# Column sums of the latent norms and of a layer norm: from fp32 columns and a root on four numbers per row to split fp32r products with ones and a root on whole tiles

## The chip, the cores and the metric

One of the eight cores of a Trainium2 chip runs the whole program in one launch. The metric is the device time of that launch in microseconds (us); lower is better. The kernel before took 3165.73 us (median of 3 runs, 3165.16 to 3166.70). Engines are named as in the profile: PE is TensorE (matmuls) and PEld its weight loads, ACT is ScalarE, DVE is VectorE, POOL is GpSimd, SP is the queue that issues most of the DMAs.

## The reference

Four blocks run one after the other on 512 positions of 1024 channels. In the first two (below: layers 0 and 1) a convolution branch is layer-normed over its 512 channels; in the last two (layers 2 and 3) an attention branch normalises two latent vectors, of 384 and of 256 channels, by their root mean square before they are projected to queries, keys and values.

```
c = causal_dwconv(glu, cf_conv_w[l], cf_conv_b[l])
c = jax.nn.silu(layernorm(c, cf_ln_g[l], cf_ln_b[l]))       # 512 channels, layers 0 and 1
...
q = (rmsnorm_2(c_q, q_norm_g) @ w_uq)                       # 384 channels, layers 2 and 3
kv = (rmsnorm_2(c_kv, kv_norm_g) @ w_ukv)                   # 256 channels
```

## The kernel before

Activations lie with channels on the 128 partitions and the 512 positions along a row, so each of these norms is a sum over partitions. `F(n)` is an fp32 tile of 128x512, `R(n)` the same room read as fp32r, the fast matmul type; `R(hi)` and `R(lo)` hold a value rounded to fp32r (`hi_part`, a CAST on ACT, L1052) and the rest (`lo_part`, a subtraction on DVE, L1455). Each weight chunk of up to 128x1024 comes by DMA into `raw`, ACT casts it into `wh` (`cut`, L977), DVE writes the rest into `wl` (`cut`, L1445), and PE then multiplies three products for each 128x128 block: high with high, high with low, low with high.

The order on each engine is the order in which its program is written. It runs over the weight chunks, and `slot(name)` marks a chunk: on ACT and on DVE it first cuts the chunk two further on (`LA`), then runs what the table `BESIDE` has for this chunk, and only then comes the chunk's own work. In layers 2 and 3 the chunks around the change are, in this order: `ckv1`, `kr`, `zb0`, `zb1`, `qr0`, `qr1`, `vb0`, `vb1`, `qk0`, `zb2`. `qr0` and `qr1` multiply the normed 384 channels, `vb0` and `vb1` the normed 256. `gate_head` takes a `zb` group through Tanh (ACT, L1233) and a product (DVE, L1832). The results of `qr0` and `qr1` are rotated: SP issues a `swap` of each (four small DMAs, L2215), but in its queue that stands behind the wait for the low part of an earlier chunk: the swaps of rows 0 and 1 wait for `vb1` to be cut. DVE multiplies what was swapped (L1687), POOL combines (L2106, L2109), and ACT and DVE split the result for `scores(0)`, the first score products of the attention.

A norm's sum before: POOL adds the squares of the tiles into one, `columns` multiplies it by a column of ones in fp32 (four matmuls with one output column each), DVE scales and adds EPS (`col`, L1460), POOL takes the power -0.5 of 4 numbers per partition (`root`, L2049), and `rows` spreads them over all partitions by four fp32 matmuls with the identity. DVE then multiplies by what lies in PSUM (L1519 for the latents, L1505 for the layer norm). The layer norm's mean is one fp32 matmul with ones.

Of the kernel before, what the change touches and what calls it, by code (L numbers as in the profile page):

```python
# [12 lines left out]
P = 128  # L13
# [334 lines left out]
BESIDE_LN = ("ln_sum", "ln_centre", "ln_root")  # L348
# [24 lines left out]
def build(nc, x_in, wst, vec, cst, tab, gmb, gains_in, out):  # L373
    ctx = ExitStack()
    with ctx:
# [14 lines left out]
        ct = sb("ct", [P, 2, P], F32)  # L390
        sm = sb("sm", [P, 160], F32)
# [3 lines left out]
        half = sm[:, 144:160]  # L395
# [104 lines left out]
        def tensor(e, w):  # L500
# [41 lines left out]
            def columns(key, tiles, wait):  # L542

                o = take(key)
                w.wait_ge(*at("landed", "cst"))
                w.wait_ge(*wait)
                last = None
                for n, a in enumerate(a[:, t * P:(t + 1) * P] for a in tiles for t in range(a.shape[1] // P)):
                    last = mm(o[:, n:n + 1], a, ones[:, 0:1], True, True)
                last.then_inc(*group_done.up(("done", key)))  # L550

            def rows(key, r, c0, n, at_col, wait):

                o = take(key)
                w.wait_ge(*at("landed", "cst"))
                w.wait_ge(*wait)
                for t in range(n):
                    last = mm(o[:, at_col + t * P:at_col + (t + 1) * P], r[:, c0 + t:c0 + t + 1].to_broadcast([P, P]),
                              ident, True, True)
                last.then_inc(*group_done.up(("done", key)))  # L560

            def small_step(what, L=None, i=None, j=None):
# [7 lines left out]
                elif what == "ln_centre":  # L570
                    o = take(("lnm", L))
                    w.wait_ge(*at("ln_sum", L))
                    mm(o, ones, F(62), True, True).then_inc(*group_done.up(("done", ("lnm", L))))
                elif what == "ln_root":
                    columns(("lcol", L), [F(62)], at("ln_added", L, 3))
                elif what == "ln_spread":
                    rows(("lrow", L), small(1), 0, NT, 0, at("root", "ln", L))
                elif what == "n_root":
                    columns(("ncol", L, i), [F(61 if i == "q" else 67)], at("n_added", L, i))
                elif what == "n_apply":  # L580
                    rows(("nrow", L, i), small(1 if i == "q" else 3), 0, NT, 0, at("root", "n" + i, L))
# [381 lines left out]
        def scalar(e, w):  # L963
# [20 lines left out]
            def small_step(what, L=None, i=None, j=None):  # L984
# [14 lines left out]
                elif what == "ln_centre":  # L999
                    for j in range(4):  # L1000
# [3 lines left out]
                        e.activation(F(62 + j), F(20 + j), ACT.Square).then_inc(*act_square.up(("ln_square", L, j)))  # L1004
# [8 lines left out]
                elif what == "n_squares":  # L1013
                    tiles, acc, tmp = ((47, 48, 49), 61, (62, 63)) if i == "q" else ((50, 51), 67, (68,))
                    for n, f in enumerate(tiles):
                        w.wait_ge(*at("copied", L, f))
                        if n == 0:
                            e.activation(F(acc), F(f), ACT.Square).then_inc(*act_square.up(("n_square", L, i, 0)))
                        else:
                            e.activation(F(tmp[n - 1]), F(f), ACT.Square).then_inc(  # L1020
# [193 lines left out]
            def mixer2(L):  # L1214
# [13 lines left out]
                def gate_head(h):  # L1228
                    key = f"{L}/zb{h}"
                    w.wait_ge(*at("done", key))  # L1230
                    if h == 7:
                        w.wait_ge(*at("done", ("ncol", L, "k")))
# [186 lines left out]
            cut(3)  # L1419
            for L in (0, 1):  # L1420
# [7 lines left out]
        def vector(e, w):  # L1428
# [28 lines left out]
            def col(key, n, D, q, event):  # L1457

                w.wait_ge(*at("done", key))
                e.tensor_scalar(q[:, 0:n], bank(key)[:, 0:n], 1.0 / D, EPS, ALU.mult, ALU.add).then_inc(  # L1460
                    *dve_col.up(event, ("free", key)))

            def small_step(what, L=None, i=None, j=None):
# [28 lines left out]
                elif what == "ln_centre":  # L1492
                    key = ("lnm", L)
                    w.wait_ge(*at("done", key))
                    for j in range(4):
                        e.scalar_tensor_tensor(out=F(20 + j), in0=bank(key), scalar=-1.0 / 512, in1=F(20 + j),
                                               op0=ALU.mult, op1=ALU.add).then_inc(
                            *dve_tile.up(("ln_centred", L, j), ("free", key)))
                elif what == "ln_root":
                    col(("lcol", L), NT, 512, small(0), ("col", "ln", L))  # L1500
                elif what == "ln_out":
                    key = ("lrow", L)
                    C, q = F(20 + i), F(63 + i % 2)
                    w.wait_ge(*at("done", key))
                    e.scalar_tensor_tensor(out=C, in0=C, scalar=vec1(L, "lng", i)[:, 0:1], in1=bank(key), op0=ALU.mult,  # L1505
                                           op1=ALU.mult).then_inc(*dve_tile.up(("ln_scaled", L, i), ("free", key)))
# [4 lines left out]
                elif what == "n_root":  # L1511
                    col(("ncol", L, i), NT, 384 if i == "q" else 256, small(0 if i == "q" else 2), ("col", "n" + i, L))
                elif what == "n_apply":
                    key = ("nrow", L, i)
                    n, src, hi, lo, tmp, gain = (3, 47, 32, 35, (64, 65, 66), "qg") if i == "q" else \
                        (2, 50, 38, 40, (55, 56), "kvg")
                    w.wait_ge(*at("done", key))
                    for k in range(n):
                        e.scalar_tensor_tensor(out=F(tmp[k]), in0=F(src + k), scalar=vec2(L, gain, k)[:, 0:1],  # L1519
                                               in1=bank(key), op0=ALU.mult, op1=ALU.mult).then_inc(  # L1520
                            *dve_tile.up(("n_scaled", L, i, k), ("free", key)))
# [865 lines left out]
```

## Time and profile before

| what | value |
|---|---|
| median of 3 runs | 3165.73 us |
| the profiled execution's own time | 3166.51 us |
| its span in the profile | 3165.1 us |
| PE busy | 3145.4 us, 99% of the span |
| DVE, ACT, POOL busy | 1833.1, 1241.2, 395.9 us |
| granted PE clock | 1.00 |

The span is from the first to the last recorded instruction; the time has 1.4 us more around it. Matmuls overlap their successors, so the cost of one to PE is the distance between the starts of two, not its recorded duration.

### The profile page before, as it was taken

How to read it: one execution, taken by the hardware profiler on the slowest of the kernel's cores; microseconds unless marked ns; L12 is line 12 of the kernel's file. 1: busy time of each engine (PE TensorE's matmuls, PEld its weight loads, DVE VectorE, ACT ScalarE, POOL GpSimd, SP SyncE). 2: the span in 40 equal slices, each digit the busy share in tenths (PEclk: the TensorE clock that was granted, in tenths of full speed). 3: DMA queues.
4: the chain of work that ended last, by engine and by line, in shares of the span. 5: the costliest groups of instructions: out<-in, count | busy, mean ns of one | idle time of the engine just before them, and what ended most of it. 6: DMA issues, size and time to landing. Idle time of an engine off the chain costs nothing.

```text
span 3165.1 us, 36907 instructions
## 1 busy us (share of the span) xinstructions
PE 3145.4 (99%) x14844; PEld 2632.5 (83%) x14844; DVE 1833.1 (58%) x2493; ACT 1241.2 (39%) x1866; POOL 395.9 (13%) x293
## 2 busy tenths in 40 slices
PE   8999999999999999999999999999999999999999
PEld 7888888888888888888888888888888888888887
DVE  5875456655687545666557643447645754344754
ACT  3332334344433234434445432226634543223742
POOL 0201212110020111111012000110011100011001
PEclk9999999999999999999999999999999999999999
DMA  4322223235432223222542222223432222222422
GB/s 163 122 93 100 93 100 107 93 111 201 149 120 100 88 99 113 94 94 100 206 139 82 86 96 91 96 93 113 129 132 72 82 93 93 87 100 94 140 98 102
DMA packets 105352, 345.47 MB, mean 109 GB/s; under 512 B 13824, under 2 KB 14080, under 8 KB 104416
## 3 DMA queue, kind: packets, MB, share of 16 engines
q1 hardware_dynamic: 101856, 328.53, 30.8%
q0 software_dynamic: 3184, 14.06, 1.2%
q8 instruction: 119, 1.95, 0.3%
q10 hardware_dynamic: 144, 0.52, 0.1%
q14 instruction: 49, 0.40, 0.0%
HBM read 324.71 MB, written 2.10 MB: 103 GB/s over the span
## 4 chain that ended last, share of the span: by engine, by line
PE 97%; DVE 1%; issue 1%; ACT 0%; DMA 0%; POOL 0%; POOLq 0%
PE ps L513 96%; PE ps L618 1%; PE ps L859 0%; DVE r L1455 0%; DVE wl L1445 0%; DMA X<-x_in 0%; POOL sm L2049 0%; ACT f L1286 0%; DVE h L1588 0%; DVE sm L1882 0%; PE ps L568 0%; DVE f L1581 0%; DVE f L1832 0%; DVE f L1892 0%; DVE r L1864 0%
## 5 line engine op out<-in xcount | busy, mean ns | idle before, releaser
L513 PE MATMUL ps<-h,wh 128*128 128x512 f32 (+1 forms) x5824 | 1703.9, 377 | 2.3 <-DVE h L1588 1.7
L513 PEld LDWEIGHTS ps<-h,wh 128*128 128x128 f32 x5824 | 1066.9, 189 | 201.5 <-issue 6.7
L513 PE MATMUL ps<-h,wl 128*128 128x512 f32 (+1 forms) x2912 | 1093.7, 376 | 0.0
L1445 DVE TENSOR_TENSOR wl<-raw,wh 128x1024 fp32r<-128x1024 f32 (+3 forms) x584 | 739.4, 1279 | 310.6 <-ACT wh L977 309.6
L977 ACT CAST wh<-raw 128x1024 fp32r<-128x1024 f32 (+2 forms) x596 | 591.3, 1004 | 705.4 <-PE ps L513 699.1
L513 PEld LDWEIGHTS ps<-h,wl 128*128 128x128 f32 x2912 | 549.3, 189 | 99.2
L513 PE MATMUL ps<-r,wh 128*128 128x512 f32 x1536 | 474.5, 390 | 0.0
L513 PEld LDWEIGHTS ps<-r,wh 128*128 128x128 f32 x1536 | 287.3, 188 | 59.0
L1052 ACT CAST r<-f 128x512 fp32r<-128x512 f32 x186 | 114.5, 620 | 495.9 <-DVE f L1785 148.5
L513 PE MATMUL ps<-r,wl 128*128 128x512 f32 x792 | 304.5, 389 | 0.0
L513 PE MATMUL ps<-wh,r 128*128 128x512 f32 x960 | 302.3, 390 | 0.3
L1675 DVE TENSOR_TENSOR f<-f,ps 128x512 f32<-128x512 f32 x96 | 66.0, 687 | 377.2 <-PE ps L513 377.1
L513 PEld LDWEIGHTS ps<-wh,r 128*128 128x128 f32 x960 | 180.2, 188 | 39.0 <-ACT r L977 1.9
L1455 DVE TENSOR_TENSOR r<-f,r 128x512 fp32r<-128x512 f32 (+1 forms) x212 | 150.3, 714 | 102.3 <-ACT r L1052 100.7
L2136 POOL TENSOR_TENSOR f<-f,f 128x512 f32<-128x512 f32 x64 | 114.5, 1790 | 746.1 <-DVE f L1675 746.1
L513 PE MATMUL ps<-wl,r 128*128 128x512 f32 x480 | 186.8, 389 | 0.0
L513 PE MATMUL ps<-r,r 128*128 128x512 f32 (+3 forms) x864 | 180.6, 361 | 0.0
L1777 DVE SCALAR_TENSOR_TENSOR f<-ps,vt,f 128x511 f32<-128x511 f32 (+1 forms) x176 | 131.4, 747 | 80.6 <-ACT f L1204 77.5
L1468 DVE SCALAR_TENSOR_TENSOR f<-f,vt,f 128x511 f32<-128x511 f32 (+26 forms) x240 | 175.3, 781 | 0.6
L513 PEld LDWEIGHTS ps<-r,wl 128*128 128x128 f32 x792 | 148.7, 188 | 31.3 <-DMA r<-r 0.3
L513 PEld LDWEIGHTS ps<-r,r 128*128 128x128 f32 x864 | 146.7, 188 | 21.6
L2161 POOL TENSOR_TENSOR f<-f,f 128x512 f32<-128x512 f32 x44 | 92.4, 2100 | 388.0 <-DVE f L1777 388.0
(155 smaller groups left out, 2099.6 us busy)
## 6 DMA issues: line engine op xcount, KB each, us to landing
raw<-wst SPq DMA_DIRECT2D x544, 512.0 KB, 3.3
raw<-wst SPq DMA_DIRECT2D x48, 320.0 KB, 2.8
r<-r SPq DMA_DIRECT2D x64, 128.0 KB, 2.3
f<-gains POOLq DMA_DIRECT2D x6, 1024.0 KB, 5.2
raw<-wst SPq DMA_DIRECT2D x20, 256.0 KB, 2.8
f<-f SPq DMA_DIRECT2D x72, 64.0 KB, 2.0
f<-tab POOLq DMA_DIRECT2D x16, 256.0 KB, 4.6
X<-x_in SPq DMA_DIRECT2D x4, 512.0 KB, 8.3
```

The costliest lines, as they stand in the source:

```text
L513: return e.matmul(o, a, b, start=start, stop=stop, skip_group_check=True)
L618: last = e.transpose(o[:, i * P:(i + 1) * P], F(H[a])[:, i * P:(i + 1) * P], ident)
L977: e.copy(h[:, 0:WIDTH[c]], raw[:, c % NRAW, 0:WIDTH[c]]).then_inc(*hi_cut.up(("hi", c)))
L1052: e.copy(r, f).then_inc(*act_hi.up(event))
L1445: e.tensor_tensor(l[:, 0:WIDTH[c]], raw[:, c % NRAW, 0:WIDTH[c]], h[:, 0:WIDTH[c]].bitcast(F32), ALU.subtract).then_inc(*lo_cut.up(("lo", c)))
L1455: e.tensor_tensor(lo, f, hi.bitcast(F32), ALU.subtract).then_inc(*dve_lo.up(event))
L1468: e.scalar_tensor_tensor(out=C, in0=F(16 + j)[:, 0:S - s], scalar=vec1(L, "cfw", 31 * j + i)[:, 0:1], in1=C, op0=ALU.mult, op1=ALU.add).th ...
L1675: e.tensor_tensor(F(M + j) if begins else q, q, bank(key), ALU.mult).then_inc(*dve_tile.up(("free", key), *events))
L1777: e.scalar_tensor_tensor(out=q[:, s:S], in0=bank(key)[:, 0:S - s], scalar=vec1(L, "fcw", 3 * (22 * m + j) + 2 - s)[:, 0:1], in1=q[:, s:S], ...
L2136: e.tensor_tensor(F(M + j), F(M + j), gate_at(L, b, j), ALU.add).then_inc(*pool_sum.up(*events))
L2161: e.tensor_tensor(F(t + 1), F(t), F(t + 1), ALU.mult).then_inc(*pool_tile.up(("f_prod", L, j)))
```

## The change

The sums over channels become products of the sum tile's high and low parts with a 128x128 tile of ones in fp32r (`spread_sum`, two matmuls of 512 columns each), which leave the sum on all partitions at once. The squares carry the 1/D already. ACT takes the square root of the whole 128x512 tile from PSUM with EPS as its bias, DVE takes the reciprocal of that tile, and the scaling on DVE reads it from SBUF. The single column matmuls, the matmuls with the identity, DVE's `col` and POOL's `root` of these norms go away; the split of each sum (one CAST on ACT, one subtraction on DVE) comes in. The layer norm's mean is summed in the same way. The table `BESIDE` has the steps at other chunks.

```
-        put(t, f"{L}/gate0_7", [[("ln_sum", L)], [], [("ln_centre", L)], [], [], [("ln_root", L)], [("ln_spread", L)]]
+        put(t, f"{L}/gate0_7", [[("ln_sum", L)], [("ln_split", L)], [("ln_centre", L)], [], [("ln_split2", L)], [("ln_root", L)], []]
...
-        put(t, f"{L}/ckv1", [[("n_squares", L, "q")], [("n_squares", L, "k")], [("n_root", L, "q")],
-                             [("n_apply", L, "q"), ("n_root", L, "k")], [("n_apply", L, "k")]])
+        put(t, f"{L}/ckv1", [[("n_squares", L, "q")], [("n_squares", L, "k"), ("n_split", L, "q")],
+                             [("n_split", L, "k"), ("n_root", L, "q"), ("n_apply", L, "q")],
+                             [("n_root", L, "k"), ("n_apply", L, "k")]])
...
+            def spread_sum(key, i, wait):
+
+                _, hi, lo = SUM_AT[i]
                 o = take(key)
...
+                mm(o, ones_r[:, :], R(hi), True, False)
+                mm(o, ones_r[:, :], R(lo), False, True).then_inc(*group_done.up(("done", key)))
...
+                elif what in ("ln_root", "n_root"):
+                    key, i = (("lrow", L), "ln") if what == "ln_root" else (("nrow", L, i), i)
+                    w.wait_ge(*at("done", key))
+                    w.wait_ge(*at("eps"))
+                    e.activation(F(SUM_AT[i][0]), bank(key), ACT.Sqrt, bias=eps).then_inc(
+                        *act_tile.up(("deviation", key), ("free", key)))
...
-            def col(key, n, D, q, event):
-
-                w.wait_ge(*at("done", key))
-                e.tensor_scalar(q[:, 0:n], bank(key)[:, 0:n], 1.0 / D, EPS, ALU.mult, ALU.add).then_inc(
-                    *dve_col.up(event, ("free", key)))
+            def root_all(key, q):
+
+                w.wait_ge(*at("deviation", key))
+                e.reciprocal(q, q).then_inc(*dve_col.up(("root",) + key))
...
-                elif what == "n_root":
-                    src, dst = (0, 1) if i == "q" else (2, 3)
-                    root(small(src), small(dst), NT, at("col", "n" + i, L), ("root", "n" + i, L))
```

ACT's program in layer 2, from the copy of `kr`'s result on. Before: the copy (`f_512_162`), the cut of `qr0`, the Tanh of `zb0`, the cut of `qr1`, the three high parts of the normed 384 channels, the Tanh of `zb1`, the cut of `vb0`.

```order
L1059 COPY f_512_162<-ps 128x512 [waits s_group_done]
L977 CAST wh<-raw 128x768 [waits s_raw0]
L1233 ACTIVATE f_512_151<-ps 128x512 [waits s_group_done]
L977 CAST wh<-raw 128x768 [waits s_raw1]
L1052 CAST r_512_56<-f_512_156 128x512 [waits s_dve_tile]
L1052 CAST r_512_64<-f_512_157 128x512 [waits s_dve_tile]
L1052 CAST r_512_69<-f_512_158 128x512 [waits s_dve_tile]
L1233 ACTIVATE f_512_163<-ps 128x512 [waits s_group_done]
L977 CAST wh<-raw 128x1024 [waits s_raw2]
```

In the changed kernel, from the same cut of `qr0` (L964 is now the cut, L1054 the high part, L1001 the root, L1235 the Tanh), up to the cut of `vb0`:

```order
L964 CAST wh<-raw 128x768 [waits s_raw0]
L1054 CAST r_512_70<-f_512_120 128x512 [waits s_pool_sum]
L1001 ACT_TABLE_LOAD
L1001 ACTIVATE f_512_62<-ps,sm 128x512 [waits s_group_done]
...
L1235 ACT_TABLE_LOAD
L1235 ACTIVATE f_512_151<-ps 128x512 [waits s_group_done]
L964 CAST wh<-raw 128x768 [waits s_raw1]
L1001 ACT_TABLE_LOAD
L1001 ACTIVATE f_512_120<-ps,sm 128x512 [waits s_group_done]
L1054 CAST r_512_70<-f_512_161 128x512 [waits s_dve_tile]
L1054 CAST r_512_74<-f_512_163 128x512 [waits s_dve_tile]
L1235 ACT_TABLE_LOAD
L1235 ACTIVATE f_512_164<-ps 128x512 [waits s_group_done]
L964 CAST wh<-raw 128x1024 [waits s_raw2]
```

The "..." are the three high parts of the 384 channels. Two roots, four loads of ACT's function tables, and the two high parts of the 256 channels now stand ahead of the cut of `vb0`; before, those two high parts came behind it. Layer 3 reads the same.

DVE's program at the same place, in the changed kernel, from the cut of `qr0` to the cuts of `vb0` and `vb1` (x2). L1459 is the low part, L1464 the reciprocal, L1527 the scaling, L1840 the product of `gate_head`.

```order
L1449 TENSOR_TENSOR wl<-raw,wh 128x768 [waits s_hi_cut]
L1459 TENSOR_TENSOR r_512_77<-f_512_120,r_512_70 128x512 [waits s_act_hi]
L1464 RECIPROCAL f_512_62<-f_512_62 128x512 [waits s_act_tile]
...
L1459 TENSOR_TENSOR r_512_65<-f_512_158,r_512_69 128x512 [waits s_act_hi]
L1840 SCALAR_TENSOR_TENSOR f_512_151<-f_512_151,ps 128x512 [waits s_act_tile]
L1449 TENSOR_TENSOR wl<-raw,wh 128x768 [waits s_hi_cut]
L1464 RECIPROCAL f_512_120<-f_512_120 128x512 [waits s_act_tile]
...
L1840 SCALAR_TENSOR_TENSOR f_512_164<-f_512_164,ps 128x512 [waits s_act_tile]
L1449 TENSOR_TENSOR wl<-raw,wh 128x1024 [waits s_hi_cut] x2
```

Before, a 128x4 TENSOR_SCALAR (L1460) stood in place of each reciprocal. Everything behind a reciprocal on DVE waits for it, the cut of `vb0` too.

## Rows read from the trace of the kernel before

**Rows 1.** The page: busy us, share of the span, instructions.

```profile
PE 3145.4 (99%) x14844; PEld 2632.5 (83%) x14844; DVE 1833.1 (58%) x2493; ACT 1241.2 (39%) x1866; POOL 395.9 (13%) x293
```

**Rows 2.** PE in time, layer 0, the layer norm's mean: start us, us.

```profile
278.12 1.02 PE L513 MATMUL ps<-f,ct 128*128 128x512 f32 x2
...
279.44 0.40 PE L513 MATMUL ps<-h,wl 128*128 128x512 f32 x1
```

**Rows 3.** PE in time, layer 2, a latent norm's columns and rows.

```profile
1657.86 0.95 PE L513 MATMUL ps<-ct,f 128*128 128x1 f32 x8
...
1659.22 0.40 PE L513 MATMUL ps<-h,wl 128*128 128x512 f32 x1
...
1670.58 0.39 PE L513 MATMUL ps<-h,wl 128*128 128x512 f32 x1
...
1671.26 0.39 PE L513 MATMUL ps<-h,wl 128*128 128x512 f32 x1
1671.85 1.13 PE L513 MATMUL ps<-ct,sm 128*128 128x128 f32 x8 [0.20 <-POOL sm L2049]
...
1673.29 0.40 PE L513 MATMUL ps<-r,wl 128*128 128x512 f32 x1
```

**Rows 4.** ACT and DVE in time, layer 0, behind the layer norm's columns.

```profile
301.99 2.00 ACT L977 CAST wh<-raw 128x1024 fp32r<-128x1024 f32 x2 [10.29 <-PE ps L513]
...
302.01 0.69 DVE L1675 TENSOR_TENSOR f<-f,ps 128x512 f32<-128x512 f32 x1 [7.22 <-PE ps L513]
```

**Rows 5.** DVE's reciprocals, by their two lines: ns min/median/max.

```profile
L1888 DVE RECIPROCAL sm<-sm x16: 177/178/179, 1710.1 to 2582.5; 128x4 f32<-128x4 f32 x16
...
L1805 DVE RECIPROCAL sm<-sm x2: 216/216/216, 1647.3 to 2416.9; 128x10 f32<-128x10 f32 x2
```

**Rows 6.** ACT in time, layer 2: a switch of function tables.

```profile
1645.28 0.21 ACT L1217 ACTIVATE sm<-vt 128x10 f32<-128x10 f32 x1
1645.50 1.28 ACT L1219 ACT_TABLE_LOAD   x1
1646.80 0.21 ACT L1219 ACTIVATE sm<-sm 128x10 f32<-128x10 f32 x1
```

**Rows 7.** Groups by line and shape: busy us, mean ns.

```profile
L1052 ACT CAST r<-f 128x512 fp32r<-128x512 f32 x186 | 114.5, 620 | 495.9 <-DVE f L1785 148.5 <-POOL f L2189 140.1 <-POOL f L2136 58.3
L1455 DVE TENSOR_TENSOR r<-f,r 128x512 fp32r<-128x512 f32 x188 | 129.9, 697 | 101.5 <-ACT r L1052 100.7 <-ACT r L1240 0.5
L1368 ACT ACTIVATE f<-ps,sm 128x512 f32<-128x512 f32 x20 | 13.8, 688 | 13.8 <-PE ps L513 7.6 <-DVE r L1455 6.1
L1508 DVE SCALAR_TENSOR_TENSOR f<-f,vt,f 128x512 f32<-128x512 f32 x8 | 6.0, 751 | 6.3 <-ACT f L1010 6.3
```

**Rows 8.** ACT and DVE in time, layer 2: the cut of `qr0`, and `vb0`'s two halves.

```profile
1658.54 0.84 ACT L977 CAST wh<-raw 128x768 fp32r<-128x768 f32 x1
...
1672.17 1.04 ACT L977 CAST wh<-raw 128x1024 fp32r<-128x1024 f32 x1
...
1673.25 1.23 DVE L1445 TENSOR_TENSOR wl<-raw,wh 128x1024 fp32r<-128x1024 f32 x1 [0.25 <-ACT wh L977]
```

**Rows 9.** SP and DVE in time, layer 2: the first swaps and what follows them.

```profile
1679.97 4.95 SPq L2215 DMA_DIRECT2D f<-f  x8
...
1683.84 0.69 DVE L1687 TENSOR_TENSOR f<-f,f 128x512 f32<-128x512 f32 x1 [0.54 <-DMA f<-f]
...
1699.02 1.28 DVE L1864 TENSOR_TENSOR r<-ps,r 128x512 fp32r<-128x512 f32 x2
```

**Rows 10.** PE in time, layer 2: the first scores, and the first values product.

```profile
1700.75 3.33 PE L513 MATMUL ps<-r,r 128*128 128x128 f32 x20
...
1717.41 1.96 PE L513 MATMUL ps<-f,f 128*128 128x512 f32 x5 [0.17 <-DVE f L1900]
```

**Rows 11.** The chain that ended last, two pieces near the program's start: start us, us.

```profile
16.35 8.52 PE ps L513 x48
...
29.74 14.62 PE ps L513 x120
```

More of the change, by code:

```diff
@@ L394, in build @@
         ident, ones = ct[:, 0, :], ct[:, 1, :]
-        half = sm[:, 144:160]
+        half, eps = sm[:, 144:152], sm[:, 152:153]
         views = {}
@@ L540, in slot @@
                     small_step(*step)
-            def columns(key, tiles, wait):
+            def spread_sum(key, i, wait):
+                _, hi, lo = SUM_AT[i]
                 o = take(key)
-                w.wait_ge(*at("landed", "cst"))
+                w.wait_ge(*at("ones_r"))
                 w.wait_ge(*wait)
[L547 to L560, printed above, removed]
+                mm(o, ones_r[:, :], R(hi), True, False)
+                mm(o, ones_r[:, :], R(lo), False, True).then_inc(*group_done.up(("done", key)))
             def small_step(what, L=None, i=None, j=None):
@@ L570, in small_step @@
                 elif what == "ln_centre":
-                    o = take(("lnm", L))
-                    w.wait_ge(*at("ln_sum", L))
-                    mm(o, ones, F(62), True, True).then_inc(*group_done.up(("done", ("lnm", L))))
+                    spread_sum(("lnm", L), "ln", at("ln_lo", L))
                 elif what == "ln_root":
-                    columns(("lcol", L), [F(62)], at("ln_added", L, 3))
-                elif what == "ln_spread":
-                    rows(("lrow", L), small(1), 0, NT, 0, at("root", "ln", L))
+                    spread_sum(("lrow", L), "ln", at("ln_lo2", L))
                 elif what == "n_root":
-                    columns(("ncol", L, i), [F(61 if i == "q" else 67)], at("n_added", L, i))
-                elif what == "n_apply":
-                    rows(("nrow", L, i), small(1 if i == "q" else 3), 0, NT, 0, at("root", "n" + i, L))
+                    spread_sum(("nrow", L, i), i, at("ns_lo", L, i))
             def h_half(B, hf, k):
@@ L1003, in small_step @@
                             w.wait_ge(*at("done", ("lnm", L)))
-                        e.activation(F(62 + j), F(20 + j), ACT.Square).then_inc(*act_square.up(("ln_square", L, j)))
+                        e.activation(F(62 + j), F(20 + j), ACT.Square, scale=512 ** -0.5).then_inc(
+                            *act_square.up(("ln_square", L, j)))
+                elif what in ("ln_split", "ln_split2"):
+                    second = what[8:]
+                    acc, hi, _ = SUM_AT["ln"]
+                    hi_part(F(acc), R(hi), at("ln_added", L, 3) if second else at("ln_sum", L), ("ln_hi" + second, L))
+                elif what in ("ln_root", "n_root"):
[4 more added lines that the diff above has]
+                        *act_tile.up(("deviation", key), ("free", key)))
+                elif what == "n_split":
+                    acc, hi, _ = SUM_AT[i]
+                    hi_part(F(acc), R(hi), at("n_added", L, i), ("ns_hi", L, i))
                 elif what == "ln_out":
@@ L1017, in small_step @@
                         if n == 0:
-                            e.activation(F(acc), F(f), ACT.Square).then_inc(*act_square.up(("n_square", L, i, 0)))
+                            e.activation(F(acc), F(f), ACT.Square, scale=D ** -0.5).then_inc(
+                                *act_square.up(("n_square", L, i, 0)))
                         else:
-                            e.activation(F(tmp[n - 1]), F(f), ACT.Square).then_inc(
+                            e.activation(F(tmp[n - 1]), F(f), ACT.Square, scale=D ** -0.5).then_inc(
                                 *act_square.up(("n_square", L, i, n)))
@@ L1231, in gate_head @@
                     if h == 7:
-                        w.wait_ge(*at("done", ("ncol", L, "k")))
+                        w.wait_ge(*at("n_scaled", L, "k", 1))
                     e.activation(F(ZB_AT[h]), bank(key), ACT.Tanh, scale=0.5).then_inc(*act_tile.up(("z_tanh", L, h)))
@@ L1419, in scalar @@
             cut(3)
+            w.wait_ge(*at("landed", "cst"))
+            e.copy(ones_r[:, :], ones).then_inc(*act_hi.up(("ones_r",)))
             for L in (0, 1):
@@ L2076, in small_step @@
                         e.tensor_tensor(F(62), F(62), F(62 + j), ALU.add).then_inc(*pool_sum.up(("ln_added", L, j)))
-                elif what == "ln_root":
-                    root(small(0), small(1), NT, at("col", "ln", L), ("root", "ln", L))
                 elif what == "n_squares":
```

34 lines of the change are left out of this document (20 added, 14 removed).

## The prediction

> **What bounds the kernel now.** I read the page first. PE is busy 3145.4 us of 3165.1 [rows 1]: everything else has under 20 us of PE's time to give back, and a change counts by two things only, the time between starts that it takes from or gives to PE's queue, and the waits that it puts there. So the next view is PE in time at the places of the change. Three products of a weight block take 0.68 us, from 1670.58 to 1671.26 [rows 3]: 0.227 us for 512 columns. That is the unit below. Then I read ACT and DVE in time around the same places, since their order decides when a sum is split and when the next weights are cut, and last the queue of SP, from which the rotation's swaps come.
>
> **What PE is spared.** Between the column product's start at 1657.86 and the next `wl` product at 1659.22 stand the column group and two products of the next group: 1.36 - 2 x 0.227 = 0.91 us [rows 3]. The spread: 1673.29 - 1671.85 - 0.45 = 0.99 us, and PE stood 0.36 us longer before it than a follow-on would (1671.85 - 1671.26 - 0.227) [rows 3]. The layer norm's mean, one fp32 product of 512 columns: 279.44 - 278.12 - 0.45 = 0.87 us [rows 2]. In their place come two fp32r products of 512 columns for each sum, 0.45 us.
> Layers 0 and 1: 0.87 + 0.91 + 0.99 - 2 x 0.45 = 1.85 us less each. Layers 2 and 3: 2 x (0.91 + 0.99 - 0.45) + 0.36, about 3.2 us less each. If nothing else moved, 10.1 us.
>
> **Layers 0 and 1: nothing gives it back.** The new work is one cast and one subtraction for the mean, the same for the variance, then a load of the root's table, the root, the load of the sigmoid's table, the reciprocal. The last four stand in the stretch behind the columns, where ACT is idle for 10.29 us and DVE for 7.22 us until PE frees them [rows 4]. ACT's stretch begins at 291.7; root and two loads take 0.69 + 2 x 1.31 = 3.3 us of it. DVE's begins at 294.8, where the root is there already, and the reciprocal takes 3.4 us of it (below). All ends before 299, and nothing is asked for until 302. The split of the variance waits for POOL's last addition and ends several us before PE asks for it. Without that cover the worst would be a wait of the 3.4 us. So these two layers give 3.7 us.
>
> **The reciprocal.** No row has one of a full tile. A tile of 4 columns takes 178 ns, one of 10 columns 216 [rows 5]: 6.3 ns a column over 153 ns. For 512 columns that gives 153 + 508 x 6.3 + 4 x 6.3, 3.4 us. From below: at the rate of DVE's other operations it would be 0.70 to 0.75 us [rows 7]. From above: if the 4 columns lie on a floor, only the 216 ns count, and with a fixed part of 130 ns they give 8.6 ns a column, 4.5 us. I take 3.4, since the fit puts its fixed part where the other operations have theirs.
> The Trainium skill, "VectorE: DVE Perf Modes" (the section on the datapath's eight slices), has the reciprocal as an iterative divide with a repeat count of 8. Read as eight cycles an element at 0.96 GHz, an estimate from that page, it is 4.3 us and more, about the upper end; the two rows give six cycles.
>
> **A switch of tables.** From the end of the activation before (1645.49) to the start of the one behind the load (1646.80) are 1.31 us [rows 6]. The Trainium skill, "ScalarE: Activation LUTs" (What ACT_TABLE_LOAD costs), adds a drain of 1.38 us to the same 1.28, 2.66 in all. The trace has no such gap behind this load; it is a rival below.
>
> **Layers 2 and 3: the chain.** In the times of before, with PE at 1657.86 when it takes up the first sum. That sum is split by then. PE's arrivals follow by counting products: `zb0`, the second sum, `zb1` make 52 with the first sum, so it asks for `qr0` at 1657.86 + 52 x 0.227 = 1669.7 (1672.8 before), and 36 products later, at 1677.8, for `vb0` (1681.0 before).
> ACT and DVE: the cut of `qr0` ends at 1659.38 [rows 8]; high part of the 256 channels' sum 0.62, table 1.31, root 0.69 (an activation from PSUM with a bias [rows 7]): 1662.0. Reciprocal 3.4: 1665.4. Three scalings at 0.75: 1667.65; three low parts at 0.70: 1669.7. `qr0` is just met. On ACT the last high part ends at 1668.3, table 1.31, Tanh at most 0.69, cut of `qr1` 0.84: 1671.1. Table 1.31, root 0.69: 1673.1. Reciprocal 3.4: 1676.5. Two scalings: 1678.0. High part 0.62, table 1.31, Tanh 0.69: 1680.6. Only now comes the cut of `vb0`: 1.04 on ACT, 1.23 on DVE [rows 8]: 1682.8. Records of neighbours on one engine overlap by 0.1 us (two low parts take 1.28 [rows 9], not 1.39), which takes about 0.4 off: **1682.4. PE waits 4.6 us**, where it had 6.5 us to spare before (DVE was done at 1674.5 [rows 8]).
> What is late next: behind the cut of `vb0` ACT copies two results and cuts `vb1`, done on DVE near 1684.3. SP's swaps of rows 0 and 1 stand behind that cut; they began at 1679.97 [rows 9], now 4.4 us later. From their landing (DVE at 1683.84) DVE is nearly without a pause up to the low parts for the first scores, 1699.02 to 1700.30 [rows 9], with PE at 1700.75 [rows 10]: slack 0.45. So scores start at about 1700.3 + 4.4 = 1704.7. PE itself, 87 products after 1682.4, is there at 1702.2, and **waits 2.5 us more**. DVE is still what PE waits for at the first values product (0.17 us before [rows 10]), so the lateness is not won back: each layer ends 4.0 us later than before, that is 7.1 of waits against 3.2 spared.
> Sum: 2 x 4.0 - 3.7 = +4.3 us. On the profiled execution's 3166.51 this is 3170.8; that execution lay 0.8 over the median, so I forecast **3170.0**, 0.14% more. What a measurement of this kernel can tell from no change is about 0.2%, 6.3 us.
> After such a wait PE may also run slower: near the start, behind its long wait, 48 products of 256 columns took 0.178 us each, later ones 0.122 [rows 11]. Six us of that would cost some 2 us, but behind `vb0` the second wait hides it, so it isn't in the sum.
>
> **The rivals.**
> 1. *The chain as worked out*, reciprocal 3.1 to 3.7 us: 3166 to 3174. The chance is 0.55. Against it: 30 links by hand; 1 us wrong in the chain is 2 us in the time.
> 2. *The reciprocal runs at DVE's usual rate.* 2.7 us less, twice per layer: `vb0` is cut at 1677.0, before PE asks. The swaps start 1.0 us earlier than before, scores at about 1699.3 (PE there at 1697.6). Each layer gains 1.45 us: 3165.7 - 3.7 - 2.9 = 3159. Against it: six columns more cost 38 ns. 0.08. The same side is reached if the swaps or ACT's order have more slack than I count: one wait of the two falls away, 3161 to 3166. 0.12.
> 3. *Slower: the reciprocal at 4.4 us or more.* Each of the two delays everything behind it on DVE, the cut of `vb0` with it: 1 us more is 2 us per layer, 3174 at 4.4 us. The point from which it decides: 3172, a reciprocal of 3.9 us. For it: a floor under the 4 columns. 0.20.
> 4. *A table switch costs 2.7 us, not 1.3.* All four per layer lie on the chain to `vb0`: 4 x 1.35 x 2 = 10.8 us, 3181. That is the page's figure; against it are the 1.31 us [rows 6]. 0.05.
>
> **How the numbers follow.** Likeliest is the first, 3170. Low end: it has to reach into the gain of rival 2, 3161; high end: rival 3 with 4.5 us and a little more, 3176. Left out are rival 4, the pure form of rival 2, and what lies beyond the ends: under 2 in 10. Faster by over 0.2% (under 3159.4): rival 2's first half and a little, 0.10. Slower (over 3172.1): rivals 3 and 4 and a quarter of the first, 0.33. Same: 0.57.
>
> **What would show it.** In layers 0 and 1 PE should have no new wait, and reach layer 2 3.7 us earlier. A RECIPROCAL of 128x512 near 3.4 us, six of them; 12 more ACT_TABLE_LOADs. PE waits before `vb0` for DVE's `wl` (4 to 5 us) and before the first scores for DVE's `r` (2 to 3 us), in both layers, and nothing at `qr0`. The forecast is wrong if no wait stands before `vb0`, if the reciprocal is under 1 or over 4 us, or if PE's waits later in the attention shrink by as much as these grow.

## The result and the profile after

| kernel | median, us | lowest to highest | runs |
|---|---|---|---|
| before | 3165.47 | 3164.67 to 3166.70 | 16 |
| changed | 3171.94 | 3170.32 to 3173.72 | 16 |

The changed kernel takes 1.0020 of the time before (95% interval 1.0014 to 1.0027), 6.5 us more. The profiled execution took 3171.99 us, its span is 3170.7 us. One later execution of the kernel before, beside the first four experiments, took 8757.54 us and is in none of the ratios.

The first part of the page of the changed kernel, to be read against [rows 1]:

```profile
PE 3140.1 (99%) x14760; PEld 2626.4 (83%) x14760; DVE 1862.5 (59%) x2502; ACT 1265.1 (40%) x1893; POOL 392.7 (12%) x287
```

PE has 84 matmuls fewer and 5.3 us less work, and the kernel is slower all the same. The view of PE's waits, summed by what ended them, says where that went (line, releaser: us in total, times, longest):

```profile
PE ps L605 <- DVE f L1589: 10.8, 2, 10.6
PE ps L517 <- DVE wl L1449: 9.3, 3, 4.5
PE ps L517 <- DVE h L1596: 2.0, 1, 2.0
PE ps L517 <- DVE r L1872: 1.8, 2, 1.0
```

The first and third stand in the program's first 20 us, before the change matters (10.7 and 1.7 us in the kernel before). The second is the cut of `vb0`, 4.5 us in each of layers 2 and 3, the fourth the first scores. DVE in time, layer 2, shows what the `vb0` cut (L1449, 128x1024) stands behind:

```profile
1657.34 3.35 DVE L1464 RECIPROCAL f<-f 128x512 f32<-128x512 f32 x1 [0.96 <-ACT f L1001]
1660.73 2.26 DVE L1527 SCALAR_TENSOR_TENSOR f<-f,vt,f 128x512 f32<-128x512 f32 x3
1662.91 1.89 DVE L1459 TENSOR_TENSOR r<-f,r 128x512 fp32r<-128x512 f32 x3
...
1668.31 3.35 DVE L1464 RECIPROCAL f<-f 128x512 f32<-128x512 f32 x1 [1.04 <-ACT f L1001]
1671.70 1.41 DVE L1527 SCALAR_TENSOR_TENSOR f<-f,vt,f 128x512 f32<-128x512 f32 x2
1673.14 1.35 DVE L1459 TENSOR_TENSOR r<-f,r 128x512 fp32r<-128x512 f32 x2
1675.71 0.69 DVE L1840 SCALAR_TENSOR_TENSOR f<-f,ps 128x512 f32<-128x512 f32 x1 [1.22 <-ACT f L1235]
1676.64 1.23 DVE L1449 TENSOR_TENSOR wl<-raw,wh 128x1024 fp32r<-128x1024 f32 x1 [0.24 <-ACT wh L964]
```

and ACT in time the other half of that chain, from the end of the first three high parts:

```profile
1663.66 1.28 ACT L1235 ACT_TABLE_LOAD   x1
...
1666.30 1.28 ACT L1001 ACT_TABLE_LOAD   x1
1667.59 0.69 ACT L1001 ACTIVATE f<-ps,sm 128x512 f32<-128x512 f32 x1
1672.49 1.28 ACT L1054 CAST r<-f 128x512 fp32r<-128x512 f32 x2 [4.21 <-DVE f L1527]
1673.79 1.28 ACT L1235 ACT_TABLE_LOAD   x1
1675.08 0.60 ACT L1235 ACTIVATE f<-ps 128x512 f32<-128x512 f32 x1
1675.57 1.04 ACT L964 CAST wh<-raw 128x1024 fp32r<-128x1024 f32 x1
```

Read the two together: each engine's bracket names the other, ACT's 4.21 us and DVE's 1.04 and 1.22. In this stretch neither runs far ahead, so what lengthens one delays the cut. The experiments below show by how much: all of a reciprocal's time counts, and of the four loads' 5.2 us only 3.65. What waits at the end of that chain is PE. PE in time, and then SP's queue and DVE behind the swaps:

```profile
1677.97 0.77 PE L517 MATMUL ps<-wh,r 128*128 128x512 f32 x1 [4.50 <-DVE wl L1449]
...
1679.81 0.63 PE L517 MATMUL ps<-wl,r 128*128 128x512 f32 x1
...
1681.09 0.63 PE L517 MATMUL ps<-wl,r 128*128 128x512 f32 x1
...
1684.12 0.39 PE L517 MATMUL ps<-wl,r 128*128 128x512 f32 x1
...
1684.81 0.39 PE L517 MATMUL ps<-wl,r 128*128 128x512 f32 x1
...
1701.37 3.42 PE L517 MATMUL ps<-r,r 128*128 128x128 f32 x20 [0.99 <-DVE r L1872]
```

```profile
1679.81 5.99 SPq L2217 DMA_DIRECT2D f<-f  x8
...
1684.82 0.69 DVE L1695 TENSOR_TENSOR f<-f,f 128x512 f32<-128x512 f32 x1 [3.70 <-DMA f<-f]
...
1699.99 1.28 DVE L1872 TENSOR_TENSOR r<-ps,r 128x512 fp32r<-128x512 f32 x2
```

Behind the wait three products take 1.28 us, from 1679.81 to 1681.09, and 3.0 us later, from 1684.12 on, three take 0.69. The view by stretches has PE's granted clock in the third column from the right, 0.50 and then 1.00, the levels 1.2 and 2.4 GHz:

```profile
1678.00:1683.00 5.00, 5.00 (x12) 3.98 (x13) 2.56 (x3) 2.72 (x5) 1.73 (x1) 0.50 0.38 112
1684.00:1690.00 6.00, 6.00 (x28) 4.95 (x27) 3.42 (x3) 3.72 (x6) 4.98 (x4) 1.00 0.61 173
```

For the sum by layers one mark serves: the first ACT instruction of an attention branch (in [rows 6] at 1645.28). In the changed kernel it is, in layers 2 and 3:

```profile
1640.69 0.21 ACT L1219 ACTIVATE sm<-vt 128x10 f32<-128x10 f32 x1
...
2415.58 0.21 ACT L1219 ACTIVATE sm<-vt 128x10 f32<-128x10 f32 x1
```

Before, layer 3's stands at 2414.92:

```profile
2414.92 0.21 ACT L1217 ACTIVATE sm<-vt 128x10 f32<-128x10 f32 x1
```

So the mark of layer 2 comes 4.6 us earlier, layer 2 itself took 5.25 us more than before and layer 3, to the end of the span, 4.95 us more: -4.6 + 5.25 + 4.95 = +5.6 us, the difference of the two spans.

### The profile page after: what moved, and what is told of

The parts are those of the page before. It is cut to its first block, busy times and chain, and to the rows that moved or that the text cites. A ratio compares the mean times of both kernels' runs of the same rounds, so it can differ in the third digit from the quotient of the medians.

```text
span 3170.7 us, 36760 instructions
## 1 busy us (share of the span) xinstructions
PE 3140.1 (99%) x14760; PEld 2626.4 (83%) x14760; DVE 1862.5 (59%) x2502; ACT 1265.1 (40%) x1893; POOL 392.7 (12%) x287
## 4 chain that ended last, share of the span: by engine, by line
PE 96%; DVE 2%; ACT 1%; DMA 0%; SPq 0%; issue 0%; POOL 0%; POOLq 0%
PE ps L517 95%; PE ps L605 1%; PE ps L846 0%; DVE wl L1449 0%; DVE f L1464 0%; DVE r L1459 0%; DVE f L1527 0%; DMA X<-x_in 0%; ACT wh L964 0%; ACT L1235 0%; ACT L1001 0%; SPq L2217 0%; ACT f L1288 0%; DVE h L1596 0%; DVE sm L1890 0%
## 5 line engine op out<-in xcount | busy, mean ns | idle before, releaser
L1449 DVE TENSOR_TENSOR wl<-raw,wh 128x1024 fp32r<-128x1024 f32 (+3 forms) x584 | 739.8, 1279 | 300.3 <-ACT wh L964 299.3
L964 ACT CAST wh<-raw 128x1024 fp32r<-128x1024 f32 (+2 forms) x596 | 591.6, 1004 | 688.0 <-PE ps L517 683.7
L1054 ACT CAST r<-f 128x512 fp32r<-128x512 f32 x194 | 119.5, 620 | 508.9 <-DVE f L1793 148.6
L1459 DVE TENSOR_TENSOR r<-f,r 128x512 fp32r<-128x512 f32 (+1 forms) x220 | 157.8, 723 | 102.2 <-ACT r L1054 101.1
```

Of the source, the lines that this page charges most:

```text
L964: e.copy(h[:, 0:WIDTH[c]], raw[:, c % NRAW, 0:WIDTH[c]]).then_inc(*hi_cut.up(("hi", c)))
L1054: e.copy(r, f).then_inc(*act_hi.up(event))
L1449: e.tensor_tensor(l[:, 0:WIDTH[c]], raw[:, c % NRAW, 0:WIDTH[c]], h[:, 0:WIDTH[c]].bitcast(F32), ALU.subtract).then_inc(*lo_cut.up(("lo", c)))
L1459: e.tensor_tensor(lo, f, hi.bitcast(F32), ALU.subtract).then_inc(*dve_lo.up(event))
```

## The experiments

Eight kernels, each timed in five rounds beside the kernel before. Ratios are to that kernel, differences "to the changed kernel" are of medians, to 3171.94. In the first four the kernel before ran 30 times with a median of 3165.57, in the last four 33 times with 3165.23.

| kernel | median (lowest to highest), us | ratio (95% interval) | profiled time, span |
|---|---|---|---|
| mix1_only | 3161.60 (3160.80 to 3162.79) | 0.9988 (0.9979 to 0.9997) | 3160.87, 3159.6 |
| no_recip | 3159.20 (3157.98 to 3159.93) | 0.9979 (0.9970 to 0.9988) | 3159.62, 3158.3 |
| no_switch | 3166.02 (3164.03 to 3168.49) | 1.0001 (0.9992 to 1.0010) | 3164.36, 3163.0 |
| reordered | 3157.14 (3156.15 to 3158.07) | 0.9973 (0.9962 to 0.9983) | 3156.94, 3155.6 |
| kept_busy | 3171.65 (3171.06 to 3173.08) | 1.0021 (1.0012 to 1.0030) | 3171.07, 3169.5 |
| swap_early | 3169.55 (3167.99 to 3169.93) | 1.0013 (1.0004 to 1.0022) | 3168.69, 3167.4 |
| busy_and_swap | 3167.09 (3166.36 to 3168.25) | 1.0006 (0.9998 to 1.0015) | 3167.09, 3165.5 |
| cut_early | 3170.85 (3168.77 to 3171.97) | 1.0018 (1.0009 to 1.0028) | 3168.77, 3167.5 |

The executions of kept_busy and cut_early overlap those of the changed kernel (3170.32 to 3173.72); the executions of the other six all lie under its fastest.

### Only layers 0 and 1 changed

The layer norm of layers 0 and 1 as in the changed kernel, the latent norms of layers 2 and 3 as before.

```
-        put(t, f"{L}/ckv1", [[("n_squares", L, "q")], [("n_squares", L, "k"), ("n_split", L, "q")],
-                             [("n_split", L, "k"), ("n_root", L, "q"), ("n_apply", L, "q")],
-                             [("n_root", L, "k"), ("n_apply", L, "k")]])
+        put(t, f"{L}/ckv1", [[("n_squares", L, "q")], [("n_squares", L, "k")], [("n_root", L, "q")],
+                             [("n_apply", L, "q"), ("n_root", L, "k")], [("n_apply", L, "k")]])
...
-                    spread_sum(("nrow", L, i), i, at("ns_lo", L, i))
+                    columns(("ncol", L, i), [F(61 if i == "q" else 67)], at("n_added", L, i))
+                elif what == "n_apply":
+                    rows(("nrow", L, i), small(1 if i == "q" else 3), 0, NT, 0, at("root", "n" + i, L))
```

> Layers 0 and 1 as in the changed kernel, layers 2 and 3 as in the kernel before. My theory (all of the loss arises in layers 2 and 3, all of the gain of layers 0 and 1 reaches the end): 3.7 us under the kernel before, about 3161.8, between 3161.3 and 3162.3, and no new wait of PE. Rival (the gain of layers 0 and 1 is partly given back later): 3164 or more.

Measured: 4.0 us faster than before, where 3.7 were forecast for this part, and PE has no new wait behind the program's first 40 us. In the changed kernel's DVE in time the reciprocal of layer 0 lies in the gap where it was put:

```profile
293.27 3.35 DVE L1464 RECIPROCAL f<-f 128x512 f32<-128x512 f32 x1
300.17 0.69 DVE L1683 TENSOR_TENSOR f<-f,ps 128x512 f32<-128x512 f32 x1 [3.55 <-PE ps L517]
```

It ends at 296.6, and DVE still waits 3.55 us for PE. The split with ones pays where its new work has such a gap; the loss lies in layers 2 and 3.

### No reciprocal in the latent norms

```
-                    root_all(("nrow", L, i), F(SUM_AT[i][0]))
+                    q = F(SUM_AT[i][0])
+                    w.wait_ge(*at("deviation", ("nrow", L, i)))
+                    e.tensor_scalar(q, q, 1.0, None, ALU.mult).then_inc(*dve_col.up(("root", "nrow", L, i)))
```

> The changed kernel with each of the four reciprocals of layers 2 and 3 replaced by a multiplication by 1 of the same tile, so that the latents are scaled by the root instead of its inverse: the values leave the reference's. My theory (the chain over both reciprocals decides when the weights of vb0 and vb1 are cut and so when the swaps start): the chain is 5.8 us shorter in each layer, PE waits for nothing before vb0, the first scores start 5.8 us earlier, still with a wait of 2 to 3 us: 3160, between 3158.5 and 3162. Rival (the reciprocals lie beside the table loads, which bound): under 2 us per layer, 3168 or more.

Measured: 12.7 us less than the changed kernel. The substitute takes 0.43 us, so each reciprocal counted 2.92 us, two in each layer: 11.7 us of chain for 12.7 us of time. DVE in time, layer 2, and PE in time, layer 3:

```profile
1665.25 0.43 DVE L1523 TENSOR_SCALAR f<-f 128x512 f32<-128x512 f32 x1 [1.04 <-ACT f L1001]
...
1670.66 1.23 DVE L1449 TENSOR_TENSOR wl<-raw,wh 128x1024 fp32r<-128x1024 f32 x1 [0.25 <-ACT wh L964]
```

```profile
2462.58 4.99 PE L517 MATMUL ps<-r,r 128*128 128x128 f32 x20 [1.72 <-DVE r L1874]
```

The cut of `vb0` begins 5.98 us sooner than 1676.64 (2 x 2.92 = 5.84), and PE no longer waits for it. The first scores still wait, 1.04 us in layer 2 and 1.72 in layer 3, less than the 2 to 3 expected. In layer 2 they start 7.2 us sooner, counted from the layer's mark, and not 5.8: the first group of swaps takes SP 4.96 us here and 5.99 in the changed kernel's trace. This is rival 2's mechanism at rival 2's size: with the reciprocals gone the new form is faster than the old by 6.4 us.

### No table switch at the latent roots

```
-                    e.activation(F(SUM_AT[i][0]), bank(key), ACT.Sqrt, bias=eps).then_inc(
+                    e.activation(F(SUM_AT[i][0]), bank(key), ACT.Sqrt if i == "ln" else ACT.Identity, bias=eps).then_inc(
```

> The changed kernel with the four roots of layers 2 and 3 replaced by an activation that every table has (Identity with the same bias), so that no table is switched there; the values leave the reference's. My theory (four switches of 1.3 us in each layer, all in the chain to vb0): 5.2 us less per layer, 3161.5, between 3160 and 3163, no wait before vb0. Rival 4 of the prediction (a switch costs 2.7 us): 10.8 us less per layer in the chain, with PE then bound by its own work, 3156 or less. Rival (the loads lie in idle time of ACT, since it waits for DVE's scaling anyway): 3168 or more.

Measured: 5.9 us less than the changed kernel, a little over half of the 10.4 expected, and outside what either rival gave. ACT and DVE in time, layer 2, show where the rest stays (of the ten loads at L1001 and L1235 two are left, those of the layer norms):

```profile
1659.78 3.11 DVE L1527 SCALAR_TENSOR_TENSOR f<-f,vt,f 128x512 f32<-128x512 f32 x3
...
1666.08 3.34 DVE L1464 RECIPROCAL f<-f 128x512 f32<-128x512 f32 x1
```

```profile
1671.92 1.04 ACT L964 CAST wh<-raw 128x1024 fp32r<-128x1024 f32 x1
```

The cut of `vb0` comes 3.65 us sooner (1671.92, was 1675.57), not 4 x 1.3 = 5.2. The first load gives 0.95 (reciprocal at 1656.39, was 1657.34), since then DVE's low part is what it waits for. Of that the three scalings take back 0.85: they last 3.11 us, not 2.26. POOL runs one operation of its own there, in POOL in time:

```profile
1659.90 1.78 POOL L2110 TENSOR_TENSOR f<-f,f 128x512 f32<-128x512 f32 x1 [7.82 <-DMA f<-f]
```

In the changed kernel it starts at 1659.83, lasts 1.29 us and overlaps the scalings by 0.4 us; here it overlaps them by 1.8, and both are longer. That the overlap is the reason is not shown: no run takes POOL's operation away, and in no_recip, where it overlaps the scalings by a few hundredths of a microsecond and then DVE's low parts, POOL's takes 3.03 us and DVE's are no longer than in the changed kernel. The second load gives 1.4 us, the third 0.7 of its 1.3 (the second reciprocal now stands directly behind DVE's cut of `qr1`, with no wait for ACT), the last 1.4: in all 0.10 + 1.4 + 0.7 + 1.4 = 3.6. So 5.2 - 3.65 = 1.55 us of each layer's expectation do not reach the cut, 3.1 us of the 4.5 missing. In layer 3 PE's clock takes some more: before the scores PE waits 2.93 us, and then the 20 score products take 4.97 us, at a granted clock of 0.66 in the mean, against 3.42 in the changed kernel's layer 2:

```profile
2467.30 4.97 PE L517 MATMUL ps<-r,r 128*128 128x128 f32 x20 [2.93 <-DVE r L1872]
```

Such slow scores lengthen a layer by about 1.0 us (the table behind the last experiment), so the expectation comes to 3161.5 + 3.1 + 1.0 = 3165.6. The profiled execution took 3164.36, 1.7 us under the median, so such a balance is good to 2 us and no better. The 1.3 us of one switch stand: an expectation with 2.7 us for each was 10 us away.

### Another order

The chain broken up by order alone, no work left out: both roots under one table load, `vb0` cut ahead of the low parts of the 256 channels, the swaps of `qr0` and `qr1` one chunk earlier. The second block of the diff is ACT's program, the third DVE's; the numbers in the first are the chunks at which the swaps are issued, counted from `kr`.

```
-    for _r, _n in enumerate((7, 8, 9, 10) if _L < 2 else (10, 10, 11, 11, 7)):
+    for _r, _n in enumerate((7, 8, 9, 10) if _L < 2 else (9, 9, 10, 10, 7)):
...
-                for h in range(2):
-                    slot(f"{L}/zb{h}")
-                    gate_head(h)
+                cut(NAME[f"{L}/zb0"] + LA)
+                small_step("n_split", L, "k")
+                small_step("n_root", L, "q")
+                small_step("n_root", L, "k")
+                small_step("n_apply", L, "q")
+                cut(NAME[f"{L}/zb1"] + LA + 1)
+                gate_head(0)
+                small_step("n_apply", L, "k")
+                gate_head(1)
...
+                slot(f"{L}/zb0")
+                cut(NAME[f"{L}/zb1"] + LA)
+                small_step("n_root", L, "k")
+                small_step("n_apply", L, "k", 0)
+                cut(NAME[f"{L}/zb1"] + LA + 1)
+                small_step("n_apply", L, "k", 1)
+                gate_head(0)
+                gate_head(1)
```

> The changed kernel with the same operations in another order in layers 2 and 3: both roots on ACT behind one table load, the Tanh of zb0 and zb1 behind one more, vb0 cut together with qr1 ahead of the 256 channels' last steps, DVE's products of the two Tanh behind them, and SP's four swaps one chunk earlier. My theory (order, not the amount of work, makes the waits): nothing waits before vb0, the first scores wait under 1 us, about 3156, between 3154.5 and 3159, faster than both kernels. Rival (the reciprocals' 6.7 us on DVE cannot be hidden before vb0, wherever they stand): PE still waits 2 us or more there, 3162 or more.

Measured: the fastest, 8.4 us under the kernel before and 14.8 under the changed one, as expected, and nothing waits before `vb0`. ACT in time, layer 2: one load serves both roots, and the Tanhs stand behind a second.

```profile
1655.19 1.28 ACT L1001 ACT_TABLE_LOAD   x1
1656.49 0.69 ACT L1001 ACTIVATE f<-ps,sm 128x512 f32<-128x512 f32 x1
1659.72 0.69 ACT L1001 ACTIVATE f<-ps,sm 128x512 f32<-128x512 f32 x1 [2.54 <-PE ps L517]
...
1665.20 1.28 ACT L1235 ACT_TABLE_LOAD   x1
```

DVE, SP's queue and PE in time: the cut of `vb0` at 1670.14, the swaps at 1671.93 instead of 1679.81, and 0.71 us as the longest wait that is left in the layer.

```profile
1670.14 1.22 DVE L1456 TENSOR_TENSOR wl<-raw,wh 128x1024 fp32r<-128x1024 f32 x1
```

```profile
1671.93 6.14 SPq L2229 DMA_DIRECT2D f<-f  x8
```

```profile
1693.77 3.41 PE L517 MATMUL ps<-r,r 128*128 128x128 f32 x20 [0.71 <-DVE r L1884]
```

Four reciprocals of 3.35 us are still on DVE in layers 2 and 3 and cost next to nothing here. So it is their place in the order that made them expensive. The edit moves three things at once (the cuts, the swaps, and the table loads, of which it needs two fewer in each layer); how the 14.8 us divide among them isn't shown. Earlier cuts alone and earlier swaps alone gave 1.1 and 2.4 us (below). The prediction's "If nothing else moved, 10.1 us" is reached but for 1.7 us, about the two waits of 0.7.

### PE kept busy ahead of `vb0`

16 products with ones, whose result is overwritten, fill most of the wait.

```
+                    if n == 0:
+                        first = take(("vb", L, 0, 0))
+                        for _ in range(16):
+                            mm(first, ones_r[:, :], R(32), True, True)
...
-                        o = take(("vb", L, n, t))
+                        o = first if (n, t) == (0, 0) else take(("vb", L, n, t))
```

> The changed kernel with 16 more products of ones with a high part (3.6 us of PE's time) ahead of the wait for vb0's weights, in layers 2 and 3, into the PSUM bank that vb0's first group then overwrites. They keep PE's clock up in the wait. My theory (the first scores start when DVE is done, and PE's 2.3 us at half rate lie in front of that): the granted clock stays at 1.00, PE waits over 3 us for the first scores instead of 1, and the time is that of the changed kernel, 3171 to 3173. Rival (the clock after the wait is part of the loss): 2 us less per layer, 3168 or less.

Measured: 0.3 us under the changed kernel, no difference. The granted clock stays at 1.00 from 1678 to 1683, where it was 0.50, but PE waits for the scores instead: 2.28 us in layer 2, 0.99 in the changed kernel (over 3 were expected):

```profile
1678.00:1683.00 5.00, 5.00 (x23) 4.12 (x24) 2.56 (x3) 3.69 (x7) 1.75 (x1) 1.00 0.42 116
```

```profile
1700.12 3.42 PE L517 MATMUL ps<-r,r 128*128 128x128 f32 x20 [2.28 <-DVE r L1876]
...
2473.83 4.99 PE L517 MATMUL ps<-r,r 128*128 128x128 f32 x20 [2.19 <-DVE r L1876]
```

In layer 3 the wait of 2.19 us is again followed by slow scores. From the layers' marks the scores start 1.15 and 0.97 us sooner than in the changed kernel's trace, about as much as the first groups of swaps are shorter (4.94 and 4.95 us, 5.99 and 5.91 there): the stretch that PE won gives nothing by itself.

### The first swaps one chunk earlier

```
-    for _r, _n in enumerate((7, 8, 9, 10) if _L < 2 else (10, 10, 11, 11, 7)):
+    for _r, _n in enumerate((7, 8, 9, 10) if _L < 2 else (9, 9, 11, 11, 7)):
```

> The changed kernel with SP's swaps of rows 0 and 1 one chunk earlier in its queue, so that they wait for vb0's low part and not for vb1's: 1.9 us earlier. My theory (the swaps decide when DVE is ready for the first scores, but PE, at half rate behind its wait, is only 1 us ahead of DVE there): 1 us less per layer, 3170, between 3169 and 3171. Rival (DVE's own work before the scores decides, not the swaps' landing): no change, 3171.5 or more.

Measured: 2.4 us under the changed kernel, in the range expected. SP's queue and PE in time, layer 2:

```profile
1677.83 4.96 SPq L2217 DMA_DIRECT2D f<-f  x8
```

```profile
1700.23 3.33 PE L517 MATMUL ps<-r,r 128*128 128x128 f32 x20
```

The swaps start behind the cut of `vb0` itself, and PE waits for the scores no more; its own slow stretch now sets their time (they started at 1701.37). In layer 3 that stretch is shorter, behind the same wait of 4.49 us: 7 products in 3.10 us and then the usual rate, and the layer is 2.1 us shorter than the changed kernel's, layer 2 only 1.2.

### Both of these

The edits of the last two kernels together.

```
+                        for _ in range(16):
+                            mm(first, ones_r[:, :], R(32), True, True)
...
-    for _r, _n in enumerate((7, 8, 9, 10) if _L < 2 else (10, 10, 11, 11, 7)):
+    for _r, _n in enumerate((7, 8, 9, 10) if _L < 2 else (9, 9, 11, 11, 7)):
```

> Both edits together: the 16 products that keep PE busy, and the swaps of rows 0 and 1 one chunk earlier. My theory: with PE at full rate the whole 1.9 us of the swaps count, perhaps 1 more where SP issues them without a pause: 2 to 3 us less per layer, 3167, between 3165.5 and 3168.5, more than the sum of the two edits alone. Rival (they add up): 3170.

Measured: 4.9 us under the changed kernel, where the two alone gave 0.3 and 2.4. The scores start at 1698.79 behind a wait of 0.70 us. Layer 2 compares the three without the swaps' own scatter, since the first group takes SP 4.94 to 4.96 us in each: counted from the layer's mark the scores start at 59.53 us in kept_busy, 59.60 in swap_early and 57.98 here. So the slow stretch and the late swaps lie beside each other, and each hides the other: either one alone gives little. A part of the 4.9 is another matter: with waits of 0.7 us the scores of layer 3 aren't slow, as they were in kept_busy.

### The cuts of `vb0` and `vb1` two steps earlier

```
                 for h in range(2):
+                    if h:
+                        cut(NAME[f"{L}/zb1"] + LA + 1)
                     slot(f"{L}/zb{h}")
                     gate_head(h)
                 for p in range(2):
+                    if p == 0:
+                        cut(NAME[f"{L}/qr0"] + LA + 1)
                     slot(f"{L}/qr{p}")
```

The same lines on ACT and on DVE.

> The changed kernel with the cut of vb0 moved to where qr1 is cut, on ACT and DVE, and that of vb1 to where vb0's was, with the switches of tables and SP's queue as they are. The wait before vb0 is then for the 256 channels' low part, about 2.2 us instead of 4.5. My theory (the swaps decide, and they start only 1.1 us earlier): 1 to 2 us less per layer, 3169, between 3167.5 and 3170.5. Rival (the wait before vb0 itself is the loss): 2.3 us or more less per layer, 3167.3 or less.

Measured: 1.1 us under the changed kernel in the medians, 0.35 beyond the range expected, and the two kernels' executions overlap. The wait ahead of `vb0` falls from 4.50 to 1.46 us and has another cause: the low parts of the 256 channels (L1463), which `vb0` needs as much as its weights. PE in time, layers 2 and 3:

```profile
1674.81 0.47 PE L517 MATMUL ps<-wh,r 128*128 128x512 f32 x1 [1.46 <-DVE r L1463]
...
1699.12 4.97 PE L517 MATMUL ps<-r,r 128*128 128x128 f32 x20 [2.99 <-DVE r L1880]
...
2472.86 3.43 PE L517 MATMUL ps<-r,r 128*128 128x128 f32 x20 [3.00 <-DVE r L1880]
```

The wait before `vb0` is 3.0 us shorter in each layer, and the slow stretch behind it is gone, but the wait for the scores grows by 2.0 and 2.2 us, for the swaps start only 1.1 us sooner (1678.73). Most of what the first wait and the stretch gave up the second wait took. The rest, 2.1 and 2.0 us of earlier scores in this trace, is the swaps' earlier start and a first group of swaps that is 1.0 us shorter (4.95 us).

In every trace the layer's length follows the start of its first scores. Both are counted from the layer's mark and set against the changed kernel (its scores start at 60.68 and 60.43 us; us, minus is sooner or shorter):

| kernel | scores of layer 2, the layer | scores of layer 3, the layer |
|---|---|---|
| before | -5.21, -5.25 | -4.96, -4.94 |
| mix1_only | -5.24, -5.33 | -4.96, -5.13 |
| no_recip | -7.17, -7.23 | -6.25, -5.22 (slow scores) |
| no_switch | -4.89, -4.87 | -3.94, -2.93 (slow scores) |
| reordered | -7.47, -7.52 | -7.34, -7.45 |
| kept_busy | -1.15, -1.11 | -0.97, +0.01 (slow scores) |
| swap_early | -1.08, -1.18 | -1.92, -2.06 |
| busy_and_swap | -2.70, -2.74 | -2.44, -2.58 |
| cut_early | -2.14, -1.08 (slow scores) | -1.96, -2.01 |

Where the 20 score products run at their usual rate the two agree within 0.2 us, so nothing behind the scores gives the delay back or adds to it. Where the products are slow (4.97 to 4.99 us instead of 3.4) the layer is 1.0 to 1.1 us longer than the start says.

## Why the prediction was right, and where it was off

3170.0 was forecast, 3171.94 measured, in the range and within the likeliest case's own (3166 to 3174). The kernel got slower, as forecast, and by the waits that were named. By the prediction's steps:

- **PE is spared 10.1 us, and layers 0 and 1 keep their part: held.** Measured 4.0 us for that part alone against 3.7. In the changed kernel's trace the mark of layer 2 is 4.6 us earlier; about 0.9 of it is there before layer 0's norm (a mark at 219.5 us came at 218.6), where no operation of the change has run yet, so the median of 4.0 is the better number.
- **The reciprocal: 3.4 us from two small tiles' slope, measured 3.35.** No floor lay under the 4 columns, and rival 3, which needed 3.9 us, falls. The prediction's estimate of 4.3 us and more, from the repeat count of 8 in the Trainium skill, "VectorE: DVE Perf Modes" (First, the fixed hardware budget), was too long; the measured row decides.
- **The table switch: 1.31 us.** From the end of the two high parts (1672.49 + 1.28) to the start of the Tanh behind the load (1675.08) it is 1.31 again. The drain of 1.38 us that the Trainium skill adds, "ScalarE: Activation LUTs" (What ACT_TABLE_LOAD costs), shows in no row here. Rival 4 falls.
- **The wait before `vb0`: 4.6 forecast, 4.50 and 4.51 measured.** Set on the prediction's clock (4.6 us added), PE takes up `vb0` at 1682.6, forecast 1682.4. SP's first swaps are 4.4 us late as forecast (1679.81 + 4.6 = 1684.4, against 1679.97 [rows 9]).
- **"So scores start at about 1700.3 + 4.4 = 1704.7": the term that was mis-sized.** They start at 1701.37 + 4.6 = 1706.0. The lateness was taken from the swaps' start, and the first of SP's swap groups took 5.99 us here, 4.95 before: DVE gets its first rows 5.0 us behind the start of the group, not 3.9 [rows 9]. That is 1.1 of the 1.3 us; DVE then needs the same 15.2 us to the low parts for the scores (1684.82 to 1699.99) as before. Each layer came out at +5.25 and +4.95 us instead of 4.0, and with layers 0 and 1 giving 0.3 to 0.9 more than forecast the sum missed by 1.3 to 1.9 us. In the experiments' layer 2 the same group takes SP 4.94 to 4.96 us in seven kernels and 6.14 in the fastest, in their layer 3 5.67 to 6.08 in four and 4.95 in four, and the kernel before has 5.99 in its second group of layer 3. So it looks like a scatter and not like a cost of the change; there is one trace of each kernel, and how often the changed kernel's other executions have the long group isn't shown.
- **"behind `vb0` the second wait hides it": held, and shown by kept_busy, but only just.** PE ran the 13 products behind the wait in 5.45 us (1677.97 to 1683.42), 13 x 0.227 = 2.95 at its usual rate: 2.5 us lost. The forecast had 2.5 us of wait to hide it in. What was left of the second wait was 0.99 and 0.80, not the 2 to 3 us named as a sign, and this much only because the swaps landed 1.1 us late; without that the slow stretch would have filled the wait to its end. That the two sizes fit was luck. Kept busy, PE lost the stretch and got the wait back, and the time stayed.
- **Not foreseen:** that a wait for the scores of 2 to 3 us can slow the score products too. In the changed kernel's own trace the waits are 0.99 and 0.80 us and the scores aren't slow, so it is no part of the 5.6 us there. Whether it is in the changed kernel's wider scatter (3.4 us from lowest to highest, 2.0 before) isn't shown.

That the chain as worked out is the cause is shown from both ends: take its two longest links away in each layer (no_recip) and 12.7 us go, re-order the work with two table loads fewer in each layer (reordered) and 14.8 us go. What stays open: why POOL's and DVE's operations were both longer in no_switch, why the first swap group sometimes takes a microsecond more, and why the same wait sometimes slows PE and sometimes doesn't.

## What to carry to other kernels

A change that takes work from the bounding engine and gives it to two idle ones is priced by where the new links stand in their order: here the same new form, reciprocals and all, made a layer 5 us longer in one order and about 2 us shorter in another ((8.4 - 4.0) / 2), on engines at 40% and 59% busy. Follow each new instruction to what stands behind it in its engine's program, and count what is late next, the DMAs in a queue that waits for it too. When a wait is removed, ask at once for the next limit: two that lie beside each other (a slow stretch and a late swap, 0.3 and 2.4 us alone, 4.9 together) have to be taken away together.

## What the runs showed of the hardware

- The granted clock fell to 0.50, and 13 products took 0.42 us each instead of 0.227, behind PE's wait of 4.5 us. Behind shorter waits it went either way: 20 score products took 4.97 to 4.99 us behind waits of 1.72, 2.19, 2.93 and 2.99 us, and 3.41 to 3.44 behind waits of 0.63 to 1.04, 2.25, 2.28 and 3.00 us. The two kinds overlap, so the length of the wait alone does not decide; what does, these runs leave open. The length of the slow stretch differs too: 13 products behind the wait of 4.50 us, 7 (in 3.10 us) behind one of 4.49 in swap_early.
- A reciprocal of 128x512 in fp32 takes 3.35 us on DVE, with 6 ns between the shortest and the longest of six. The straight line through 4 and 10 columns gave 3.4.
- A group of eight swap DMAs takes SP 4.95 us or 5.7 to 6.1, the same code in the same place: of the first groups of layers 2 and 3 in all ten traces, 7 of 20 took the longer time.
